# A hybrid decoder step: reordered beginning, first expert block by one-hot products, reordered end

## The reference, cut to what matters

```python
mem_k, mem_v = mem_kv_projection(mem_prompt, g_mem, w_mem_kv)   # 256 memory tokens, both layers
# layer 0
h = rmsnorm(x, g_pre_mix[0]); proj = h @ w_in_a; ga, gb, qm = split(proj)
u = ga * sigmoid(gb); u_ext = concatenate([conv_prev, u])       # conv_prev: zeros, or state_conv for decode
o = silu(layernorm(depthwise_conv31(u_ext, conv_w) + conv_b))
x += rmsnorm(concat(o, mem_attention(qm, mem_k, mem_v)) @ w_out_a) ; x += rmsnorm(swiglu(rmsnorm(x)))
k, v = split(rmsnorm(x, g_kv) @ w_kv)                           # shared K/V
# layer 1: stick-breaking attention (sb_bias, paged cache through page_table) and memory attention
# then top-2-of-8 experts
h = rmsnorm(x, g_pre_ffn[1]); logits = h @ w_router + b_router
gates = top2(softmax(logits)); f = sum_e gates[e] * swiglu(h, wg[e], wu[e], wd[e])
x += rmsnorm(f, g_post_ffn[1])
```

## Time and profile before

| | |
|---|---|
| profiled execution, its own time | 1896.83 us |
| its span | 1894.4 us |
| median of three runs | 1898.61 us |
| PE busy | 1694.3 us (89%) |
| DVE busy | 965.1 us (51%) |
| ACT busy | 727.7 us (38%) |
| POOL busy | 588.8 us (31%) |

### The profile page before, as it was taken

How to read it: one execution, slowest core, us unless ns; L and a number is a source line. 1 busy time by engine, 2 the same in 40 slices (tenths; PEclk the granted TensorE clock), 3 DMA queues, 4 the chain that set the end, 5 groups by cost and what they waited for, 6 DMA issues and landing times.

```text
span 1894.4 us, 28758 instructions
## 1 busy us (share of the span) xinstructions
PE 1694.3 (89%) x11174; PEld 1528.2 (81%) x11174; DVE 965.1 (51%) x1127; ACT 727.7 (38%) x948; POOL 588.8 (31%) x332
## 2 busy tenths in 40 slices
PE   4898887899999997889899995699999999999991
PEld 4798667899999997889665593589898998989880
DVE  5897544311111004231684417467586775867755
ACT  4445443222222123122553313345454444544542
POOL 3333222255554342232000122242241423314232
PEclk8899898999999998999799997799999999999996
DMA  5424202144445232122534216669789697887924
GB/s 166 127 89 141 67 10 80 41 143 139 138 138 183 84 128 89 45 89 68 202 117 139 67 34 190 186 207 290 194 238 245 200 298 195 257 226 219 261 94 163
DMA packets 347699, 283.41 MB, mean 150 GB/s; under 512 B 11747, under 2 KB 311823, under 8 KB 347497
## 3 DMA queue, kind: packets, MB, share of 16 engines
q1 hardware_dynamic: 327845, 253.54, 46.1%
q10 hardware_dynamic: 16532, 16.57, 2.6%
q0 software_dynamic: 3264, 12.50, 1.7%
HBM read 248.19 MB, written 35.10 MB: 150 GB/s over the span
## 4 chain that ended last, share of the span: by engine, by line
PE 42%; issue 27%; POOL 12%; DVE 11%; ACT 4%; DMA 2%; SPq 2%; POOLq 0%; DVEq 0%; ACTq 0%
PE ps L2111 33%; POOL ea L837 9%; DVE cT L1476 3%; PE ps L2239 2%; POOL ea L839 1%; PE ps L2073 1%; DVE rstd L1323 1%; PE ps L2429 1%; PE ps L2136 1%; POOL wlo L724 1%; DVE zc L1791 1%; PE ps L2249 1%; DMA tmp<-in_conv_w 1%; PE ps L2063 1%; PE ps L2480 1%
## 5 line engine op out<-in xcount | busy, mean ns | idle before, releaser
L2602 PE MATMUL ps<-ejx,ewh 128*128 128x384 f32 x1408 | 405.3, 362 | 3.3 <-issue 1.9
L1970 DVE TENSOR_TENSOR ewl<-eraw,ewh 128x2048 fp32r<-128x2048 f32 (+1 forms) x144 | 303.9, 2112 | 185.7 <-ACT ewh L1254 185.4
L1254 ACT ACTIVATE ewh<-eraw 128x2048 fp32r<-128x2048 f32 (+1 forms) x144 | 255.2, 1773 | 311.2 <-PE ps L2605 168.4
L2111 PE MATMUL ps<-hh,whi 128*128 128x260 f32 x1504 | 315.7, 292 | 50.2 <-DVE hl L1706 27.5
L2605 PE MATMUL ps<-ejx,ewl 128*128 128x192 f32 x1408 | 353.9, 251 | 0.0
L837 POOL TENSOR_TENSOR ea<-eat,ea 128x128 fp32r<-128x128 f32 x88 | 181.7, 2065 | 433.6 <-ACT ea L1278 433.6
L2111 PE MATMUL ps<-hh,wlo 128*128 128x260 f32 x1504 | 308.4, 287 | 0.0
L2111 PE MATMUL ps<-hl,whi 128*128 128x260 f32 x1504 | 308.3, 287 | 0.0
L2111 PEld LDWEIGHTS ps<-hh,whi 128*128 128x128 f32 x1504 | 239.8, 194 | 55.4 <-issue 32.7
L730 POOL TENSOR_TENSOR wlo<-raw,whi 128x2048 fp32r<-128x2048 f32 x46 | 214.9, 4671 | 211.0 <-ACT whi L860 87.2
L2602 PEld LDWEIGHTS ps<-ejx,ewh 128*128 128x128 f32 x1408 | 265.9, 189 | 6.7 <-issue 6.7
(11 more groups left out here) (378 smaller groups left out, 2648.6 us busy)
## 6 DMA issues: line engine op xcount, KB each, us to landing
eraw<-in_w_gate_e SPq DMA_DIRECT2D x88, 512.0 KB, 4.8
eraw<-in_w_up_e SPq DMA_DIRECT2D x88, 512.0 KB, 6.2
eraw<-in_w_down_e SPq DMA_DIRECT2D x64, 512.0 KB, 5.7
eraw<-in_w_down_e SPq DMA_DIRECT2D x48, 256.0 KB, 2.7
xs<-zero ACTq DMA_DIRECT2D x10, 1152.0 KB, 4.8
raw<-in_w_gate_d SPq DMA_DIRECT2D x22, 512.0 KB, 4.0
raw<-in_w_up_d SPq DMA_DIRECT2D x22, 512.0 KB, 5.2
raw<-in_w_down_d SPq DMA_DIRECT2D x16, 512.0 KB, 4.3
```

The source lines that it names most:

```text
L1254: e.activation(ewh[:, s, 0:n], eraw[:, u % RAW, 0:n], ACT.Copy).then_inc(ew_hi, 1)
L1970: e.tensor_tensor(ewl[:, s, 0:n], eraw[:, u % RAW, 0:n], ewh[:, s, 0:n].bitcast(F32), ALU.subtract)\
L2111: ins = e.matmul(ps[:, 2 * q + h, 0:HALF], w, xx[:, k, h * HALF:(h + 1) * HALF], start=opens, stop=closes)
L2602: e.matmul(ps[:, q, 0:2 * C], ewh[:, s, o:o + P], ejx[:, k, :, :].rearrange("p h n -> p (h n)"), start=(k == 0), stop=(k == KD - 1), skip_ ...
```

## The change

In the beginning all lists are put in another order. On SP's queue the third weight chunk goes ahead of `crow_raw`, the fourth behind it, and the two first chunks of `w_in_a` ahead of the state rows. The four small tables go to POOL's queue, and `crow_raw` gets a place of its own (it lay in `tmp` before). ACT does `mem_high(1)` and `hi_of(2)` where it copied `crow_raw`, and copies that in the middle of `norm_high`. DVE does `mem_low(1)` early, the x tiles and the diagonal next, and the copies of the turned taps last. PE multiplies the diagonal straight behind the x transposes, then the memory tiles, then the taps; the state rows are turned behind the loop of the projection, and DVE copies them behind the last pair.

In the experts, DVE makes a table `oh` after the slots are known: for each token a row of 192 columns with the token's norm factor in the column of its slot in block 0. PE multiplies the tokens `xtk` (not normed, token-major) by it, which gives block 0 turned, normed and gathered at once; ACT and DVE multiply by the gain as they split it. The reading of block 0 from DRAM is dropped, the scatter is not. Three of the four zeroing products move ahead of the counting products.

At the end ACT takes half of the copies of the last block, the root's table is loaded ahead, the gain row is loaded before the loop of the blocks, and the tile of 8 rows is taken first.

```diff
@@ SP
-            e.dma_start(ptab[:, :], ...).then_inc(small_in, 16)      # and bias, wr, br
-            for g in range(2, 4):
-                e.wait_ge(w_lo, g - 1)
-                load_whole(g % 2, a["w_mem_kv"][1], (g - 2) * NMEM)
+            e.wait_ge(w_lo, 1)
+            load_whole(0, a["w_mem_kv"][1], 0)
             e.wait_ge(u_zero, 1)
             for s in range(PH):
                 e.dma_start(crow_raw[...], a["conv_w"][0][:, FN * P:]).then_inc(cw_in, 16)
+            e.wait_ge(w_lo, 2)
+            load_whole(1, a["w_mem_kv"][1], NMEM)
+            for p in range(2):
+                e.wait_ge(w_lo, U_IN + p - 1)
+                load_pair((U_IN + p) % 2, win, (FS + p) * P, win, p * P)
             e.wait_ge(tp_done, TP_ST)
...
@@ POOL
-            e.memset(crow_raw, 0.0).then_inc(u_zero, 1)
+            e.dma_start(ptab[:, :], ...).then_inc(small_in, 16)      # and bias, wr, br
             e.wait_ge(const_ready, 16)
+            e.wait_ge(tp_done, TP_MEM + 4)
+            e.wait_ge(mem_step, MEM_SS)
+            e.memset(crow_raw[:, :], 0.0).then_inc(u_zero, 1)
...
             e.wait_ge(xs_in, 160)
-            e.dma_start(gtok[:, 0, :], xs[C:C + P, :]).then_inc(g0_in, 16)
-            e.dma_start(gtok[0:CB, 1, :], xs[C + P:2 * C, :]).then_inc(g0_in, 16)
...
-            for i in range(NT + 1):
+            for i in TAIL:                                           # [NT, 0, 1, 2, 3]
@@ ACT
             hi_of(1)
-            e.wait_ge(cw_in, 96)
-            e.activation(crow4, crow_raw, ACT.Copy).then_inc(cw_row, 1)
+            mem_high(1)
+            hi_of(2)
             e.wait_ge(x_in, 80)
...
-            for k in range(6):
+            for k in range(3):
                 norm_high(k)
             hi_of(4)
-            for k in range(6, KD):
+            norm_high(3)
+            e.wait_ge(cw_in, 96)
+            e.activation(crow4, crow_raw, ACT.Copy).then_inc(cw_row, 1)
+            for k in range(4, KD):
                 norm_high(k)
...
+            def first_rows_hi(c):
+                e.wait_ge(er_done, c + 1)
+                for k in range(2):
+                    kk = 2 * c + k
+                    ins = e.activation(ejx[:, kk, 0, :], ps[...], ACT.Copy, scale=gT[:, G_PRE_FFN + 8 + kk:...])
+                ins.then_inc(ej_hi, 1)
...
+                    if first and u == 2:
+                        e.wait_ge(xs_in, 160)
...
+            for n in range(2):
+                e.activation(etok[0:CB, 1, 512 * n:512 * n + 512], ps[P - CB:P, 4 + n, :], ACT.Copy).then_inc(ey_low, 1)
+            e.activation(etok[:, 0, 512:1024], ps[:, 3, :], ACT.Copy).then_inc(ey_ready, 1)
+            e.preload_act_table(ACT.Sqrt)
@@ DVE
+            link(e.tensor_tensor(own_slot[:, :], slf[:, 0, :], slf[:, 1, :], ALU.min))
+            for i in range(NT + 1):
+                e.tensor_scalar(oh[0:n, i, :], colf[0:n, :], own_slot[0:n, i:i + 1], rs[0:n, i:i + 1],
+                                ALU.is_equal, ALU.mult).then_inc(oh_ready, 1)
             row_out(1)
@@ PE
+            for c in range(4):
+                q = EB[eb_at(2 * KE + c)[0]]
+                for k in range(2):
+                    kk = 2 * c + k
+                    for i in range(NT + 1):
+                        if c == 0 and k == 0:
+                            e.wait_ge(oh_ready, i + 1)
+                        ins = e.matmul(ps[:, q, k * C:(k + 1) * C], xtk[0:n, i, kk * P:(kk + 1) * P], oh[0:n, i, :],
+                                       start=(i == 0), stop=(i == NT), skip_group_check=True)
+                ins.then_inc(er_done, 1)
+            zero_rows(3).then_inc(ed_done, 1)
...
-            rows_in(g0_in, 32, None)
```

More of the change, by code:

```diff
@@ L348, in build @@
         eb_free = [sem(f"eb_free{i}") for i in range(4)]
+        TAIL = [NT] + list(range(NT))
         yr_in = [sem(f"yr_in{i}") for i in range(NT + 1)]
@@ L1617, in _ @@
                 conv_taps(13)
+            state_columns()
             conv_decode()
@@ L2211, in _ @@
                     mem_tile(g, t)
+            e.wait_ge(cw_in, 96)
+            fill(TP_CW, [(bank(TP_CW)[:, 93 * i:93 * i + 93], crow[0:93, i, :]) for i in range(2)])
+            e.wait_ge(cw_row, 1)
+            for n in range(2):
+                f = TP_W + n
+                w = NW * PH
+                fill(f, [(bank(f)[:, w * q:w * q + w], crow4[:, (8 * n + q) * P:(8 * n + q + 1) * P]) for q in range(8)])
+            with e.Fori(0, 3) as i:
+                for j in range(2):
+                    chunk_tiles(U_IN + j, M_IN + 2 * j, i, 2, 4, ready=inputs(T_N0) if j == 0 else None)
             e.wait_ge(state_in, 32)
@@ L2216, in _ @@
                           sttok[0:4 * PAST, i, (2 * c + h) * P:(2 * c + h + 1) * P]) for h in range(2) for i in range(2)])
-            with e.Fori(0, 3) as i:
-                for j in range(2):
-                    chunk_tiles(U_IN + j, M_IN + 2 * j, i, 2, 4, ready=inputs(T_N0) if j == 0 else None)
             chunk_tiles(U_QM, M_QM, 0, 0, 0)
```

184 lines of the change are left out of this document (100 added, 84 removed).

## The result

The changed kernel takes 1882.78 us, the median of four runs (1878.76 to 1885.48), against 1899.13 for the one before in the same session (1898.02 to 1901.97). The ratio is 0.9918, 95% interval 0.9904 to 0.9931; measured once more later it was 0.9932 (0.9918 to 0.9945). So the change gives 13 to 15.5 us. The forecast was a gain of 27 (1872, range 1865 to 1883). The sign is right and the gain too large by 11 to 14; the 1882.78 lies at the slow edge of the stated range. Two of the three signs by which the prediction called itself wrong came: the projection starts after 68 (70.5), and the one-hot products take over 20 us (21.4). The third did not: the blocks' length changed by 4, not by over 5.

What follows compares the result with a forecast made beforehand. Time was sought where PE is not dense: up to 75 us, 1163 to 1206, and the end, where DVE is the chain. Gains 8 + 17 + 2 = 27 took the span from 1894.4, giving a median of 1872, range 1865 to 1883.

Steps and rivals of the forecast that it cites:

- three signs: Prediction wrong if projection starts after 68, one-hot products take over 20 us, or the blocks' length changes by over 5.
- Small tables on POOL's queue: Beginning: moving the tables costs nothing; up to 3 us lost if they delay first weights, 1 gained if they free queues.
- DVE's chain from the first normed tile: Beginning: DVE's list from the first normed tile at 43.6 takes 18.5 us, to 62.1, with the projection at 63.3.
- State transposes, +2.4 (0 to 4.6): Beginning: behind the projection loop nothing hides the state transposes on PE, so 2.4 us slower, bounds 0 and 4.6.
- So I carry the 8 through.: After the beginning: its net gain of about 8 us at the projection is kept to the end of the kernel.
- First block, 17 (4 to 20): Experts' first block: expert products start 14.5 us earlier, and 2.5 more come from the clock; 17 gained, bounds 4 and 20.
- One-hot products 16.2 with 6 us at half clock: First block: eighty PE instructions, 18 at half clock in 6 us and 62 at 0.165, take 16.2 us.
- The 3 for the clock at the experts' start: First block: expert products follow a busy PE, so their half-clock stretch goes; 3 us gained, less 0.5 for doubt.
- Rival (a): First block: one-hot products stay slow, at half clock to the end or with slow DVE splits; gain 5, 1884; chance 0.11.
- End, 2 (0 to 4): End: split copies, small tile first and a shorter DVE chain, less a larger last store, gain 2 us, bounds 0 and 4.
- Rival (b): Beginning: state rows hold SP, late stores delay POOL's sixth chunk, PE waits; gain 1 instead of 8, 1879; chance 0.17.
- Rival (c): Blocks: the chip grants PE a lower clock after the filled rest; at 0.92 the kernel takes 1909; chance 0.04.

Runs made afterwards that it cites:

- tables_late: The changed kernel with the four small tables sent by SP near 180 us instead of by POOL at 4.3; 0.9906 of the kernel before.
- beginning_alone: The kernel before with only the beginning's edits: order of all engines, tables on POOL's queue, state transposes behind the loop; ratio 1.0002.
- onehot_alone: The kernel before with only the one-hot first block of the experts; ratio 0.9952.
- busy_pe_gaps_mem: tables_late plus zero products in PE's idle stretches, three of them before the second layer's memory attention; 0.9805 of the kernel before.

## Why the prediction was wrong, step by step

**Small tables on POOL's queue: the step that failed first.** The prediction put them at nothing, with "1 more" if they free the queues, from the row in which SP's issues are short of work. They cost the beginning alone 5.5, of the 8 that it was to give. I had priced an issue and not the transfer. No row of before showed a broadcast on POOL's queue, so the rule was to bound it from both sides, and I gave it an upper gain and no loss. All dates behind it were late: third chunk sent at 23.1 (17.8 in tables_late), diagonal at 46.3 (40.3), first normed tile at 49.9 (43.6). With the tables out of the way these dates are right: 40.5 and 44.7.

**DVE's chain from the first normed tile, 18.5.** It took 19.2 with the loads late (49.88 to 69.11), and 21.2 in tables_late. The missing term is POOL's fifth chunk, 4.0 to 4.3 on one DVE instruction. I had asked when that chunk is ready, not whom it stops. That 19.2 stands so near 18.5 is luck: the terms named for it (18.2 less 2.3, plus 3, plus 1.9) make 20.8 and not 18.5; in the changed kernel the waits for memory tiles are nothing, in tables_late 1.7.

**State transposes, +2.4 (0 to 4.6): mis-sized.** Measured alone +5.1. PE's part was right: the traces show 2.3 of it and nothing else. The small copy, pushed by 2.2 into POOL's chunk (4.07 instead of 0.17), is off the path. What the other 2.7 are stays open.

**"So I carry the 8 through."** No row was behind this. In the profile of beginning_alone the lead is 4.8 at 1029 us and 0.0 at 1053: it meets the load of the cached keys, and then a PE at half clock.

Together: the gain of 8 in the sum, less 5.5 for the tables, less 2.7 for the state rows, is 0; beginning_alone measured -0.4 (-2.7 to 1.9). These are differences of runs; that they fit proves no cause. If the terms add, the new order by itself, with neither, would be 0.9973 - 0.0027, 10 us, near the 10.2 at the projection that the forecast works with (11.2 less 1). That kernel was not run, and since the traces lose a lead on the way, the agreement may be chance.

**First block, 17 (4 to 20): mis-sized by the clock.** This is the step that cost as much as the tables. The start at 1173.8 was right (1175.3 in an execution that was 1.3 behind). One-hot products 16.2 with 6 us at half clock: measured 21.4, with 11 us at half clock. These 5.2 are all that is missing: 17 less 5.2 is 11.8, and the trace gives 12 (10 in onehot_alone, where the half clock lasted 15 us; 9.1 by its ratio, 6.5 to 11.6). The rows of the experts' start were the wrong likeness: there the gap was one, here PE has two short ones and between them 2.9 us of small products. The price at half clock was right (12 in 4.00 are 0.33), that at full clock too low (0.20 with the pauses, not 0.165). The 3 for the clock at the experts' start came: no half-clock stretch at 1198.65. Rival (a), half clock to the end, had 5 for the block and 1884 for the whole, at 0.11: its time is the nearest to the measured one, its block is too poor (9.1 alone, 12 in the whole), since the half clock held for half of the products and not for all. With the beginning at nothing, which (a) does not have, its time is near by luck.

**End, 2 (0 to 4): right**, measured 3.4 (1.3 to 5.5); its chain of 18.1 was 18.3. The evictions over two engines gave 2.05 (the lead grows from 14.45 to 16.5 there), 2.0 was forecast. From the last DVE instruction to the end of the span it is 3.3 (2.2 before), 1.1 more where 1.7 was forecast.

**Rival (b)**, the beginning given back by SP: its chain is there word for word, the state rows hold SP until 70.61, the stores land at 78.4, POOL begins its sixth chunk at 78.62 (74.52 before). But PE did not wait: its row at 70.51 is followed by work without a gap until 100. The beginning was given back, for other reasons. **Rival (c)**, a lower clock in the blocks: no; their length changed by 4, in the good direction.

The page "SBUF — State Buffer" of the Trainium skill ("SBUF: two separate sides") calls the ports shared by DVE and GpSimd a lock for whole instructions. The rows above agree, down to a copy of 16 columns that took 4.07. They add that copies from `ps` to `udec` were not held: three of the six ran beside the same POOL chunk, and all six took 0.40. The page "ScalarE: Activation LUTs" of the Trainium skill ("What ACT_TABLE_LOAD costs") puts a drain of about the same length beside the load of 1.28. No row of before or after shows it: before, the square root starts at 1874.95, right behind the load from 1873.66; after, ACT was waiting for rows anyway.

## What to carry to other kernels

Moving a DMA to an idle queue is no free move: price its transfer. Where many small pieces on POOL's queue read the same bytes, keep them away from loads that somebody waits for. When an engine is moved earlier or later, ask which of the other engine's long instructions it now runs into; here three short DVE instructions were held 4 us each in this way, and two of them lay on the path. An early start is worth something only if nobody downstream waits for a load that has its own date. Ahead of a dense stretch of PE, two idle gaps of 2.5 us cost more than the gaps themselves: 6.4 us in slower products behind them. Harmless products, counted in instructions and shorter than the gap, took this away; the two kernels with them are 9 to 11 us faster. The kernel made of these steps, busy_pe_gaps_mem, takes 1859.2 (1856.1 to 1866.3): 0.9805 of the kernel before, 0.988 of the changed one.
